# Two projections go token tile by token tile, ScalarE's rounding moves, GpSimd makes some remainders

## The chip, the core and the metric

The kernel runs on one core of a Trainium2 chip. A core has a matrix engine (TensorE, PE in the rows; its weight loads are PEld), a vector engine (VectorE, DVE), an activation engine (ScalarE, ACT), a general engine (GpSimd, POOL) and a sync engine (SyncE, SP) that issues most transfers. The metric is the device time of one execution in microseconds, the median of three runs.

## The reference, cut to what matters

A first block (mixer, memory attention, 32 experts, a final rmsnorm) is followed by a second block of two layers. All tensors are 256 tokens by 1024 features.

```python
x = first_block(...)              # ends with x + moe_ffn(h), then rmsnorm(x, norm_final)
for layer in range(2):
    shift, scale, gate = ada_modulation(c, ada_w[layer, 0], ada_b[layer, 0])
    h = x * (1.0 + scale) + shift
    if layer % 2 == 0:
        y = mixer_ab(h, ...)      # begins with h @ w_in, 1024 x 1224
    else:
        y = mixer_c(h, ...)       # begins with h @ w_in, 1024 x 3072
    x = layer_norm(DN_ALPHA * x + gate * y, ...)
    shift, scale, gate = ada_modulation(c, ada_w[layer, 1], ada_b[layer, 1])
    h = x * (1.0 + scale) + shift
    y = squared_relu_mlp(h, mlp_w1[layer], mlp_w2[layer])
    x = layer_norm(DN_ALPHA * x + gate * y, ...)
```

The change touches the two lines `h @ w_in`. In the kernel the four uses of a modulated `h` are counted 0 to 3: the first (`a` = 0, "m0", weights `ab_in`), the MLP of layer 0 (1), the third (`a` = 2, "m2", weights `c_in`) and the last MLP (3).

## The kernel before

The 256 tokens are two token tiles t of 128, the 1024 features eight chunks k of 128. A product in full precision is made of three products of rounded numbers: each operand is split into a rounded part ("hi", type fp32r) and a remainder ("lo" = value minus hi), and `three` (L1185 is its matmul line) adds hi·hi, hi·lo and lo·hi into one PSUM bank.

**Weights** stream in granules of 2 MB through a ring of slots. ScalarE makes the rounded part (`split_hi`, L535) and VectorE the remainder (`split_lo`, L545); the counts w_hi and w_lo tell TensorE what is ready. `ab_in` is three granules: chunks 0 to 2, 3 to 5, and 6 and 7. The first granule's remainder is made in three pieces of 1224 columns by VectorE (`ab_in_lo`, L2271). `c_in` is six granules of four chunks; the first projection of m2 uses granules 0 and 1.

**Activations.** When the normalized X of a token tile is there (`xhat`), `transpose_hat` (L1689) turns 8 chunks of it on TensorE; the banks 4 to 7 hold two chunks of both tiles each, so a bank is complete only with the second tile. Then `evac_hi` on ScalarE (L960) makes the modulated and rounded part XT_r, one instruction of 256 columns for a chunk, and `evac_lo` on VectorE the remainder: two instructions from bank and XT_r into sb_XN (L2461), two from sb_XN into the remainder's place (L2466), four times. A chunk's matmuls wait for both.

**Around m0.** Behind the last expert ScalarE rounds `ab_in` 0, loads the table for the square root (L915), rounds `ab_in` 1, and then squares and sums X tile by tile (L919, L922). VectorE first adds the experts' banks to X (L2262), then makes the first piece of remainder, then 1/root and the scaled X (L2277, L2278: `xhat`), and further pieces between the rest. `keep_busy(0, 2)` (L1176) are matmuls without use.

**Around m2.** `layer_norm(1, ...)` on VectorE is, for each tile and half, bank times gate (L2411), plus X (L2412: both inputs in SBUF), statistics (L2413), and then small ones that alternate with ScalarE's root (L940). The first tile is scaled by ScalarE (`ln_hat`, L947), the first half of the second by VectorE (L2422). ScalarE rounds `c_in` 1 before the layer norm's first root; VectorE makes the remainders of `c_in` 1 to 3 behind `evac_lo(2)`.

The order on every engine is that of the code; semaphores join the engines. GpSimd is idle between 276.13 us, its last instruction of the routing, and 1246.25 us.

## Time and profile before

| | us |
|---|---|
| median of three runs | 1863.99 (1863.71 to 1864.62) |
| the profiled execution | 1861.1, of which its trace spans 1859.3 |
| TensorE busy | 1760.3 (95%) |
| VectorE busy | 741.1 (40%) |
| ScalarE busy | 533.5 (29%) |
| GpSimd busy | 28.1 (2%) |
| m0: from the last expert's last ScalarE instruction to the end of the projection | 1193.75 to 1238.10 |
| m2: from the end of the MLP's matmuls to the end of the first two `c_in` granules | 1525.11 to 1555.65 |

Shares over the whole span hide the two stretches; they are read from timelines of single engines, where each row gives its start, how long the group took, and, in brackets, how long the engine had been idle and who ended that. The chain of waits says which of the engines decides the end.

### The profile page before, as it was taken

The page shows a single profiled execution, that of the slowest core. Times are in us where ns is not written, and L with a number is a line of the kernel's source. Part 1 is how long each engine was busy: PE and PEld are TensorE (multiplying, and loading weights), DVE is VectorE, ACT ScalarE, POOL GpSimd, SP SyncE. Part 2 cuts the span into 40 slices and gives each one's busy share as a digit, 9 for nine tenths or more (in the row PEclk, how much of TensorE's full clock was granted, in tenths as well). Part 3 has the DMA queues.
Part 4 walks back from the last instruction along what each step waited for, and adds up shares of the span by engine and source line. Part 5 has one row for each costly group of instructions (what it writes and reads, how often), then busy time and mean ns, then how long its engine had stood idle before and what let it go on. Part 6 is the DMA issues. An engine that isn't in the chain of part 4 may idle for free.

```text
span 1859.3 us, 24433 instructions
## 1 busy us (share of the span) xinstructions
PE 1760.3 (95%) x9970; PEld 1105.8 (59%) x9970; DVE 741.1 (40%) x1253; ACT 533.5 (29%) x693; POOL 28.1 (2%) x33
## 2 busy tenths in 40 slices
PE   6999999999999999999999999798899999989997
PEld 6787774344344343443434434375699878679986
DVE  3245352122122121221212212278865568675545
ACT  4344430110110110101111010327544452644442
POOL 0101000000000000000000000000000000000001
PEclk9999999999999999999999999998999999999999
DMA  9767799999999999999999999954345555435550
GB/s 328 286 234 273 278 374 427 428 428 428 428 429 429 429 428 429 429 429 429 429 429 428 429 429 429 413 213 179 114 178 184 200 185 191 171 114 181 180 203 23
DMA packets 96698, 587.60 MB, mean 316 GB/s; under 512 B 7118, under 2 KB 7332, under 8 KB 71044
## 3 DMA queue, kind: packets, MB, share of 16 engines
q1 hardware_dynamic: 95348, 582.12, 77.4%
q10 hardware_dynamic: 1296, 4.72, 0.8%
q8 instruction: 39, 0.64, 0.1%
q14 instruction: 15, 0.12, 0.0%
HBM read 585.77 MB, written 1.05 MB: 316 GB/s over the span
## 4 chain that ended last, share of the span: by engine, by line
PE 73%; DMA 19%; DVE 4%; ACT 3%; issue 1%; SPq 0%; ACTq 0%; DVEq 0%
PE bank L1185 35%; DMA ring<-in_w_gate_up 18%; PE bank L1468 15%; PE bank L1487 8%; PE bank L1426 4%; PE bank L1498 1%; PE bank L1274 1%; PE bank L1460 1%; ACT arena L899 1%; PE bank L1480 1%; PE bank L1259 1%; PE bank L1646 1%; PE bank L1633 0%; PE bank L1388 0%; PE bank L1828 0%
## 5 line engine op out<-in xcount | busy, mean ns | idle before, releaser
L1468 PE MATMUL bank<-ring,arena 128*64 128x512 f32 x2048 | 463.1, 598 | 27.4 <-DMA ring<-in_w_gate_up 26.9
L1468 PEld LDWEIGHTS bank<-ring,arena 128*64 128x64 f32 x2048 | 138.1, 137 | 319.8 <-issue 258.0
L1185 PE MATMUL bank<-w_hi,arena_r 128*128 128x512 f32 (+1 forms) x784 | 257.4, 390 | 4.7 <-DVE arena_r L2312 2.8
L1487 PE MATMUL bank<-ring,arena 128*64 128x512 f32 x1024 | 226.8, 595 | 3.4
L545 DVE TENSOR_TENSOR w_lo<-ring,w_hi 128x4096 fp32r<-128x4096 f32 (+2 forms) x43 | 188.1, 4375 | 53.1 <-ACT w_hi L535 50.9
L535 ACT ACTIVATE w_hi<-ring 128x4096 fp32r<-128x4096 f32 (+2 forms) x45 | 159.0, 3572 | 45.5 <-DMA ring<-in_c_w_out 25.5
L897 ACT ACTIVATE arena<-arena,sb_tab 128x512 f32<-128x512 f32 x32 | 23.1, 722 | 513.3 <-DVE arena L2167 513.3
L1185 PEld LDWEIGHTS bank<-w_hi,arena_r 128*128 128x128 f32 x784 | 147.7, 188 | 35.2 <-DVE arena_r L2312 3.3
L2167 DVE TENSOR_SCALAR arena<-bank 128x512 f32<-128x512 f32 x32 | 22.1, 692 | 366.7 <-PE bank L1468 366.7
L1487 PEld LDWEIGHTS bank<-ring,arena 128*64 128x64 f32 x1024 | 72.0, 137 | 137.6 <-issue 132.7
L1185 PE MATMUL bank<-XT_r,w_hi 128*128 128x256 f32 x512 | 146.6, 286 | 4.4 <-DVE arena_r L2466 4.4
L1185 PE MATMUL bank<-arena_r,w_hi 128*128 128x256 f32 x512 | 145.6, 284 | 0.0
L1185 PE MATMUL bank<-XT_r,w_lo 128*128 128x256 f32 x512 | 145.5, 284 | 0.0
L1426 PEld LDWEIGHTS bank<-arena,sb_XN 128*128 128x128 f32 x1056 | 123.2, 192 | 26.0 <-issue 26.0
L1426 PE MATMUL bank<-arena,sb_XN 128*128 128x64 f32 x1056 | 128.4, 275 | 0.0
L1185 PE MATMUL bank<-w_lo,arena_r 128*128 128x512 f32 x320 | 125.0, 391 | 0.0
L2188 DVE SCALAR_TENSOR_TENSOR arena_r<-bank,sb_att,arena_r 128x512 fp32r<-128x512 f32 x32 | 24.0, 751 | 217.4 <-ACT arena_r L902 217.4
L1185 PEld LDWEIGHTS bank<-XT_r,w_hi 128*128 128x128 f32 x512 | 98.9, 193 | 5.8 <-issue 5.3
L1185 PEld LDWEIGHTS bank<-arena_r,w_hi 128*128 128x128 f32 x512 | 99.0, 193 | 0.9 <-issue 0.5
L1185 PEld LDWEIGHTS bank<-XT_r,w_lo 128*128 128x128 f32 x512 | 98.9, 193 | 0.0
L902 ACT ACTIVATE arena_r<-bank,sb_att 128x512 fp32r<-128x512 f32 x32 | 22.0, 687 | 231.2 <-PE bank L1487 231.2
L522 DVE TENSOR_TENSOR half_lo<-ring,half_hi 128x2048 fp32r<-128x2048 f32 x24 | 55.0, 2291 | 82.7 <-ACT half_hi L512 82.6
(389 smaller groups left out, 2104.4 us busy)
## 6 DMA issues: line engine op xcount, KB each, us to landing
ring<-in_w_gate_up SPq DMA_DIRECT2D x128, 2048.0 KB, 32.0
ring<-in_w_down SPq DMA_DIRECT2D x64, 2048.0 KB, 35.3
ring<-in_mlp_w SPq DMA_DIRECT2D x32, 2048.0 KB, 8.3
ring<-in_ada_w SPq DMA_DIRECT2D x22, 2048.0 KB, 12.5
ring<-in_c_w_in SPq DMA_DIRECT2D x6, 2048.0 KB, 7.6
ring<-in_w_in SPq DMA_DIRECT2D x4, 2048.0 KB, 9.9
ring<-in_w_k SPq DMA_DIRECT2D x2, 2048.0 KB, 12.4
ring<-in_w_v SPq DMA_DIRECT2D x2, 2048.0 KB, 8.7
```

Of the source, the lines that this page charges most:

```text
L522: eng.tensor_tensor(lo[:], half_raw(name, h)[1], hi[:].bitcast(F32), ALU.subtract).then_inc(sem("w_lo"), 1)
L535: act.activation(pair(g)[0][:, 0:w], slot(slot_of(g), w), ACT.Copy).then_inc(sem("w_hi"), 1)
L545: eng.tensor_tensor(lo[:, 0:w], slot(slot_of(granule_no(name, i)), w), hi[:, 0:w].bitcast(F32), ALU.subtract).then_inc(sem("w_lo"), 1)
L897: act.activation(sig, gcl, ACT.Sigmoid, bias=zero, scale=1.702).then_inc(sem("e_sig"), 1)
L899: act.activation(hT, B[0][:].rearrange("p (c n) -> p c n", c=4), ACT.Copy).then_inc(sem("e_hTe"), 1)
L902: act.activation(y_hi, B[2][:], ACT.Copy, scale=slot_gate).then_inc(sem("e_y"), 1)
L1185: mm = pe.matmul(out, st[a], mv[b], start=start and a + b == 0, stop=stop and a == 1, skip_group_check=True)
L1426: mm = pe.matmul(B[3][:, k * CAP:(k + 1) * CAP], XN[:, t, k * P:(k + 1) * P], sel_tok[:, t, :], start=(t == 0), stop=(t == 1))
L1468: mm = pe.matmul(B[m][CAP * h:CAP * h + CAP, :], xe[:, 2 * j + kl, :], w[:, kl, m * D + h * HW:m * D + (h + 1) * HW], start=False, stop=(j ...
L1487: mm = pe.matmul(B[2][CAP * h:CAP * h + CAP, :], hT[:, c, CAP * j:CAP * j + CAP], w[:, c, h * HW:(h + 1) * HW], start=(j == 0 and c == 0), ...
L2167: dve.tensor_scalar(gcl, B[0][:], 7.0, None, ALU.min).then_inc(sem("e_clamp"), 1)
L2188: dve.scalar_tensor_tensor(y_lo, B[2][:], slot_gate, y_hi.bitcast(F32), ALU.mult, ALU.subtract).then_inc(sem("e_ylo"), 1)
```

## The change

For m0 and for m2's first two granules, tile 0 is transposed alone into banks 4 and 5 (`transpose_tile`), and its two kinds of evacuation are made for it alone, 128 columns each (`evac_tile`). TensorE then runs, for a granule and tile 0, all hi·hi products, all with the weights' remainder, and last those with the activations' remainder; between the second and the third comes the transposing of tile 1 into banks 6 and 7, once (`project_tiles`). In m0 tile 1's outputs take banks 4 and 5, so TensorE waits there until tile 0's remainders are all made.

ScalarE no longer rounds `ab_in` 0 inside the last expert; the expert loop runs all 32. It loads the square root's table, rounds two thirds of `ab_in` 0, does the squares, rounds the last third, evacuates tile 0, rounds `ab_in` 1, and evacuates tile 1. In m2 four of tile 0's evacuations stand before tile 1's root. The five first pieces of `ab_in`'s remainder (granule 0 and two thirds of granule 1) are GpSimd's, the sixth VectorE's behind both tiles. The remainder of `c_in` 1 is GpSimd's in one instruction of 4096 columns. `keep_busy(0, 2)` ahead of m0 is `keep_busy(0, 5)`.

```diff
+        def ab_in_lo(eng, k):
+            g = granule_no("ab_in", k // 3)
+            n, cut = split_no(g), slice(k % 3 * 1224, (k % 3 + 1) * 1224)
+            hi, lo = pair(g)
+            if k < 2:
+                eng.wait_ge(sem("ab_in_hi"), 1)
+            else:
+                eng.wait_ge(sem("w_hi"), n)
+            eng.wait_ge(sem("w_lo"), n - 1)
+            ins = eng.tensor_tensor(lo[:, cut], slot(slot_of(g))[:, cut], hi[:, cut].bitcast(F32), ALU.subtract)
+            ins.then_inc(*((sem("w_lo"), 1) if k % 3 == 2 else (sem("ab_in_part"), 1)))
...
+            for k in range(5):
+                ab_in_lo(pool, k)
             pool.wait_ge(sem("late_read"), 1)
...
+            split_lo(pool, "c_in", 1)
             pool.wait_ge(sem("late_read"), 3)
...
-            expert(NE - 1, (used, MOE_END), ("ab_in", 0))
...
             act.activation(stat[:, 59:60], eps5, ACT.Sqrt, bias=zero)
-            split_hi(act, "ab_in", 1)
...
+            ab_in_hi(0, 2)
             for t in range(TB):
                 act.wait_ge(sem("moe_x"), 2 * t + 2)
...
-            evac_hi(0)
+            ab_in_hi(2, 3)
+            evac_tile(0, 0, range(KC))
+            split_hi(act, "ab_in", 1)
+            evac_tile(0, 1, range(KC))
             split_hi(act, "ab_in", 2)
...
             ln_hat(1, 0)
+            evac_tile(2, 0, range(4))
             ln_root(1, 1)
             ln_hat(1, 1)
-
-            evac_hi(2)
+            evac_tile(2, 0, range(4, KC))
+            evac_tile(2, 1, range(KC))
...
+                for t in range(TB):
+                    for wa in range(2):
+                        for kl in range(len(ks)):
+                            term(t, 0, wa, kl)
+                    if t == 0 and second is not None:
+                        second()
+                    for kl in range(len(ks)):
+                        mm = term(t, 1, 0, kl)
+                    if t == 0 and second is not None:
+                        pe.wait_ge(*upto(f"m{a}", "xt_v", KC))
+                mm.then_inc(used, 1)
...
-            keep_busy(0, 2)
-            transpose_hat(0)
+            keep_busy(0, 5)
+            transpose_tile(0, 0)
...
+                if j:
+                    pe.wait_ge(sem("w_lo"), split_no(g))
+                if j == 1:
+                    pe.wait_ge(sem("ab_in_part"), 4)
...
-            ab_in_lo(0)
             for t in range(TB):
                 dve.wait_ge(*upto("fin", "root", t + 1))
                 link(dve.reciprocal(stat[:, 80 + t:81 + t], stat[:, 18 + t:19 + t]))
                 dve.tensor_scalar(X[:, t, :], X[:, t, :], stat[:, 80 + t:81 + t], None, ALU.mult).then_inc(
                     sem("xhat"), 1)
-            ab_in_lo(1)
...
+            def evac_tile(a, t):
+                g1, g0 = modcol(a)
+                for q in range(2):
+                    dve.wait_ge(*upto(f"m{a}", "xt_a", KC * t + 4 * q + 4))
+                    for k in range(4 * q, 4 * q + 4):
+                        if t:
+                            dve.wait_ge(*upto(f"m{a}", "xt_v", k + 1))
+                        ins = dve.scalar_tensor_tensor(XN[:, 0, k * P:(k + 1) * P], B[4 + 2 * t + q][:, k % 4 * P:k % 4 * P + P],
+                                                       g1(k), XT_r[:, k, t * P:(t + 1) * P].bitcast(F32), ALU.mult,
+                                                       ALU.subtract)
+                    link(ins)
+                    for k in range(4 * q, 4 * q + 4):
+                        dve.tensor_scalar(XTL[a][:, k, t * P:(t + 1) * P], XN[:, 0, k * P:(k + 1) * P], g0(k), None,
+                                          ALU.add).then_inc(sem("xt_v"), 1)
...
-            evac_lo(0)
-            split_lo(dve, "ab_in", 1)
+            for t in range(TB):
+                evac_tile(0, t)
+            ab_in_lo(dve, 5)
             rope_angles()
...
-            evac_lo(2)
-            for i in range(1, 4):
+            for t in range(TB):
+                evac_tile(2, t)
+            for i in range(2, 4):
                 split_lo(dve, "c_in", i)
```

ScalarE behind the experts in m0, the program before. w_hi_49, w_hi_51 and w_hi_53 are the rounded parts of `ab_in` 0, 1 and 2.

```order
L535 ACTIVATE w_hi_49<-ring 128x3672
...
L915 ACT_TABLE_LOAD
L915 ACTIVATE sb_stat<-sb_tab 128x1
L535 ACTIVATE w_hi_51<-ring 128x3672
L919 ACTIVATE sb_XN,sb_stat<-sb_X,sb_tab 128x1024
L922 ACTIVATE sb_stat<-sb_stat,sb_tab 128x1
L919 ACTIVATE sb_XN,sb_stat<-sb_X,sb_tab 128x1024
L922 ACTIVATE sb_stat<-sb_stat,sb_tab 128x1
L960 ACTIVATE XT_r<-bank,sb_mod 128x256 x8
L535 ACTIVATE w_hi_53<-ring 128x2448
```

The same place on ScalarE, the changed program (its line numbers are those of the changed kernel; L936 is `ab_in_hi`, L993 `evac_tile`).

```order
L929 ACT_TABLE_LOAD
L929 ACTIVATE sb_stat<-sb_tab 128x1
L936 ACTIVATE w_hi_49<-ring 128x2448
L942 ACTIVATE sb_XN,sb_stat<-sb_X,sb_tab 128x1024
L945 ACTIVATE sb_stat<-sb_stat,sb_tab 128x1
L942 ACTIVATE sb_XN,sb_stat<-sb_X,sb_tab 128x1024
L945 ACTIVATE sb_stat<-sb_stat,sb_tab 128x1
L936 ACTIVATE w_hi_49<-ring 128x1224
L993 ACTIVATE XT_r<-bank,sb_mod 128x128 x8
L535 ACTIVATE w_hi_51<-ring 128x3672
L993 ACTIVATE XT_r<-bank,sb_mod 128x128 x8
L535 ACTIVATE w_hi_53<-ring 128x2448
```

Of 7344 rounded columns ahead of the first square, 2448 are left there; 1224 stand behind the squares, and 3672 between the two tiles' evacuations.

VectorE in m0, the program before (L2271 are the pieces of remainder, L2278 is `xhat`).

```order
L2262 TENSOR_TENSOR sb_X<-bank,sb_X 128x512 x4
L2271 TENSOR_TENSOR w_lo_50<-ring,w_hi_49 128x1224
L2277 RECIPROCAL sb_stat<-sb_stat 128x1
L2278 TENSOR_SCALAR sb_X<-sb_X,sb_stat 128x1024
L2277 RECIPROCAL sb_stat<-sb_stat 128x1
L2278 TENSOR_SCALAR sb_X<-sb_X,sb_stat 128x1024
L2271 TENSOR_TENSOR w_lo_50<-ring,w_hi_49 128x1224
L2461 SCALAR_TENSOR_TENSOR sb_XN<-bank,sb_mod,XT_r 128x256 x2
L2466 TENSOR_SCALAR arena_r<-sb_XN,sb_mod 128x256 x2
L2271 TENSOR_TENSOR w_lo_50<-ring,w_hi_49 128x1224
```

The same place on VectorE, the changed program.

```order
L2340 TENSOR_TENSOR sb_X<-bank,sb_X 128x512 x4
L2344 RECIPROCAL sb_stat<-sb_stat 128x1
L2345 TENSOR_SCALAR sb_X<-sb_X,sb_stat 128x1024
L2344 RECIPROCAL sb_stat<-sb_stat 128x1
L2345 TENSOR_SCALAR sb_X<-sb_X,sb_stat 128x1024
L2524 SCALAR_TENSOR_TENSOR sb_XN<-bank,sb_mod,XT_r 128x128 x4
L2529 TENSOR_SCALAR arena_r<-sb_XN,sb_mod 128x128 x4
```

The pieces of remainder have left this queue; the evacuations follow `xhat` directly, four of each kind in a row.

GpSimd between the routing and the last layer norm, the difference of the two programs.

```order
+L744 TENSOR_TENSOR sb_mod<-sb_mod,sb_col 128x8
+L559 TENSOR_TENSOR w_lo_50<-ring,w_hi_49 128x1224 x3
+L559 TENSOR_TENSOR w_lo_52<-ring,w_hi_51 128x1224 x2
+L750 TENSOR_TENSOR sb_mod<-sb_mod,sb_ada_bT 128x8
+L752 TENSOR_TENSOR sb_mod<-sb_mod,sb_ada_bT 128x16
+L754 TENSOR_TENSOR sb_stat<-sb_mod,sb_col 128x8
+L756 TENSOR_TENSOR sb_mod<-sb_mod,sb_stat 128x8
+L757 TENSOR_TENSOR sb_mod<-sb_mod,sb_col 128x8
+L545 TENSOR_TENSOR w_lo_54<-ring,w_hi_53 128x4096
+L760 TENSOR_TENSOR sb_mod<-sb_mod,sb_ada_bT 128x8
```

Five subtractions of 1224 columns and one of 4096 have come in between the small ones that were there.

## Rows read from the trace of the kernel before

**Rows 1.** The page: its chain of waits by engine, whole span.

```profile
PE 73%; DMA 19%; DVE 4%; ACT 3%; issue 1%; SPq 0%; ACTq 0%; DVEq 0%
```

**Rows 2.** Chain of waits, both projections: start us, us, what ran, count.

```profile
1212.86 25.24 PE bank L1185 x135
...
1531.98 67.15 PE bank L1185 x288
```

**Rows 3.** Timeline of ScalarE, first projection: start us, us, engine, line, tiles, count.

```profile
1193.75 0.69 ACT L902 ACTIVATE arena_r<-bank,sb_att 128x512 fp32r<-128x512 f32 x1 [7.25 <-PE bank L1487]
1194.34 3.26 ACT L535 ACTIVATE w_hi<-ring 128x3672 fp32r<-128x3672 f32 x1
1197.61 1.28 ACT L915 ACT_TABLE_LOAD   x1
...
1199.11 3.25 ACT L535 ACTIVATE w_hi<-ring 128x3672 fp32r<-128x3672 f32 x1
1202.26 1.13 ACT L919 ACTIVATE sb_XN<-sb_X,sb_tab 128x1024 f32<-128x1024 f32 x1
...
1207.35 3.75 ACT L960 ACTIVATE XT_r<-bank,sb_mod 128x256 fp32r<-128x256 f32 x8 [2.08 <-PE bank L1689]
1210.95 2.28 ACT L535 ACTIVATE w_hi<-ring 128x2448 fp32r<-128x2448 f32 x1
```

**Rows 4.** Timeline of VectorE, the same stretch.

```profile
1196.83 2.48 DVE L2262 TENSOR_TENSOR sb_X<-bank,sb_X 128x512 f32<-128x512 f32 x4 [1.60 <-PE bank L1498]
1199.23 1.42 DVE L2271 TENSOR_TENSOR w_lo<-ring,w_hi 128x1224 fp32r<-128x1224 f32 x1
...
1204.05 0.75 DVE L2278 TENSOR_SCALAR sb_X<-sb_X,sb_stat 128x1024 f32<-128x1024 f32 x1
...
1208.40 0.88 DVE L2461 SCALAR_TENSOR_TENSOR sb_XN<-bank,sb_mod,XT_r 128x256 f32<-128x256 f32 x2 [0.80 <-ACT XT_r L960]
1209.32 0.62 DVE L2466 TENSOR_SCALAR arena_r<-sb_XN,sb_mod 128x256 fp32r<-128x256 f32 x2
```

**Rows 5.** Timeline of TensorE, the same stretch.

```profile
1196.66 1.98 PE L1176 MATMUL bank<-sb_tab 128*128 128x512 f32 x4
1204.86 3.50 PE L1689 MATMUL bank<-sb_tab,sb_X 128*128 128x128 f32 x16 [6.21 <-DVE sb_X L2278]
```

**Rows 6.** Windows: stretch, length, busy times of engines, granted clock (PEclk), DMA, GB/s.

```profile
1204.80:1209.80 5.00, 3.50 (x16) 3.27 (x17) 3.63 (x8) 2.89 (x9) 0.00 (x0) 0.68 0.92 340
...
1533.00:1534.00 1.00, 1.00 (x4) 0.71 (x4) 1.00 (x4) 1.00 (x2) 0.00 (x0) 0.50 0.00 0
```

**Rows 7.** GpSimd: one group of the groups by line, then its timeline.

```profile
L522 POOL TENSOR_TENSOR half_lo<-ring,half_hi 128x2048 fp32r<-128x2048 f32 x4 | 18.4, 4602 | 165.4 <-ACT half_hi L512 165.4
...
1848.93 2.36 POOL L746 TENSOR_TENSOR sb_X<-sb_X,arena 128x1024 f32<-128x1024 f32 x1 [216.35 <-ACT sb_X L947]
1851.37 2.67 POOL L748 TENSOR_TENSOR sb_X<-sb_X,arena 128x1024 f32<-128x1024 f32 x1
```

**Rows 8.** Timeline of VectorE in the last 10 us, beside GpSimd.

```profile
1849.78 0.69 DVE L2411 TENSOR_TENSOR sb_XN<-bank,sb_XN 128x512 f32<-128x512 f32 x1 [0.22 <-PE bank L1185]
1850.51 1.33 DVE L2412 SCALAR_TENSOR_TENSOR sb_X<-sb_X,sb_XN 128x512 f32<-128x512 f32 x1
...
1853.50 1.08 DVE L2428 SCALAR_TENSOR_TENSOR sb_X<-sb_X,sb_att,arena 128x512 f32<-128x512 f32 x1
```

**Rows 9.** Third projection: timelines of ScalarE, of VectorE, of TensorE.

```profile
1514.51 3.61 ACT L535 ACTIVATE w_hi<-ring 128x4096 fp32r<-128x4096 f32 x1
...
1517.97 0.69 DVE L2412 SCALAR_TENSOR_TENSOR sb_X<-sb_X,sb_XN 128x512 f32<-128x512 f32 x1
...
1520.59 0.69 DVE L2412 SCALAR_TENSOR_TENSOR sb_X<-sb_X,sb_XN 128x512 f32<-128x512 f32 x1
...
1528.39 0.54 DVE L2422 TENSOR_SCALAR sb_X<-sb_X,sb_att 128x512 f32<-128x512 f32 x1
...
1525.11 1.03 PE L1689 MATMUL bank<-sb_tab,sb_X 128*128 128x128 f32 x8
```

More of the change, by code:

```diff
@@ L892, in _, with expert @@
             ada(1)
-            def expert(i, down_done, ahead=None):
+            def expert(i, down_done):
                 act.wait_ge(sem("e_clamp"), 2 * i + 1)
@@ L1694, in transpose_hat, with transpose_tile, project_tiles, term @@
                         keep_busy(0, 3)
+            def transpose_tile(a, t):
+                st = "fin" if a == 0 else f"ln{a - 1}"
+                if a == 0:
+                    pe.wait_ge(*upto(st, "xhat", t + 1))
+                elif t == 0:
+                    pe.wait_ge(*upto(st, "xhat_a", 1))
+                else:
+                    pe.wait_ge(*upto(st, "xhat", 1))
+                for k in range(KC):
+                    if a and t == 1 and k == 4:
+                        pe.wait_ge(*upto(st, "xhat_a", 2))
+                    mm = pe.transpose(B[4 + 2 * t + k // 4][:, k % 4 * P:k % 4 * P + P], X[:, t, k * P:(k + 1) * P], ident)
+                    if k % 4 == 3:
+                        mm.then_inc(sem("T"), 1)
+            def project_tiles(a, g, w, ks, outs, width, second=None, w_ready=None):
+                def term(t, xa, wa, kl):
+                    k = ks[kl]
+                    pe.wait_ge(*upto(f"m{a}", ("xt_a", "xt_v")[xa], KC * t + k + 1))
+                    if t + xa == 0 and w_ready is not None:
+                        w_ready(wa, kl)
+                    x = (XT_r, XTL[a])[xa]
+                    for c, b in enumerate(outs[t]):
+                        mm = pe.matmul(b, x[:, k, t * P:(t + 1) * P], w[wa][:, kl, width * c:width * c + width],
+                                       start=k + xa + wa == 0, stop=xa == 1 and k == KC - 1, skip_group_check=True)
+                    return mm
+                for t in range(TB):
[9 more added lines that the diff above has]
+                mm.then_inc(used, 1)
             def x_chunk(a, k):
```

72 lines of the change are left out of this document (34 added, 38 removed).

## The prediction

> **What bounds the kernel now.** I read the chain of waits first: TensorE holds 73% of it [rows 1], and in both places that the change touches the chain lies on the projection's matmuls once they run: 135 of the 144 of m0 from 1212.86 to 1238.10, 0.187 us each, and 288 of m2 from 1531.98, 0.233 us each [rows 2]. Their number does not change, so a gain can come only from an earlier start or fewer gaps. Ahead of them the bound is a relay, read from the timelines. In m0 it runs: the last expert's end 1194.44, rounding of `ab_in` 0 for 3.26, table 1.28, rounding of `ab_in` 1 for 3.25, first square at 1202.26 [rows 3]; then root, `xhat` at 1204.05 on VectorE [rows 4], transposing at 1204.86 [rows 5], evacuation from 1207.35. In m2 it is VectorE's layer norm up to 1528.93, then transposing and evacuation until 1531.98 [rows 9, 2].
>
> **m0, ScalarE.** Without the two roundings ahead, the table load follows the last expert at about 1195.0 (0.5 us for the count that it must read, an estimate), ends 1196.3, the root's warm-up 1196.5, two thirds of `ab_in` 0 (2448 columns cost 2.28 [rows 3]) 1198.8. The first square can start then: its X half tiles are added by 1198.1 (two of the four of 2.48 us [rows 4]). So 1198.7 against 1202.26: **3.5 us earlier**. The last third of `ab_in` 0 stands behind the second root, 1201.6 to 1202.8. Evacuating costs 0.46 us per 256 columns (3.75 for 8); 128 columns lie between half and all of that; I take 0.35, so 2.9 us a tile, as the fixed part weighs more than the columns. Rounding `ab_in` 1 between the tiles costs 3.26 and ends about 1209.0.
>
> **m0, without a collision.** The relay's fixed distance from square to transposing is 2.6 us (1202.26 to 1204.86), so transposing at 1201.3. The longer `keep_busy` (10 instructions; 4 cost 1.98 [rows 5], so 4.6) ends by 1201.2 and is hidden in the wait; would X come earlier, it would cost the overlap. TensorE then works on hi·hi and hi·lo of tile 0, waits for GpSimd's third piece, and would end about 1233.0: **5.1 us gained**, if GpSimd and VectorE ran side by side.
>
> **GpSimd's price, and whom it stops.** A GpSimd subtraction of 2048 columns costs 4.60, one of 1024 costs 2.36 [rows 7]: 1224 cost 2.8, 4096 cost 9.1. VectorE pays 1.42 for 1224 [rows 4]. But the last 10 us of the trace show more. VectorE's L2412, with two SBUF inputs, takes 0.69 everywhere [rows 9], yet 1.33 at 1850.51, and ends at 1851.84: GpSimd's first operation ran until 1851.29 [rows 7, 8]. L2428 takes 1.08 and ends 1854.58, GpSimd's second having ended at 1854.04. Both end 0.55 behind GpSimd, which is their own streaming: they stood still until it was through. The second GpSimd operation is 0.31 longer than the first, since it in turn met the running L2412. L2411, from a bank and one SBUF tile, ran in the middle of it in 0.69: not stopped. So **two-input SBUF operations of VectorE and GpSimd exclude each other for a whole instruction**. L2278 and L2466 have one SBUF tile as input; no row shows them beside GpSimd. L2278 makes 1024 columns in 0.75, twice the rate per column of L2271, so it must move two columns at a time; I take it and L2466 as stopped too, and the bound on the other side is that they are not (a rival).
>
> The page "SBUF — State Buffer" of the Trainium skill, section "SBUF: two separate sides", says that the pair of ports that GpSimd and VectorE share is an exclusive lock, held for the whole instruction, and that a VectorE operation in a 2-port performance mode takes it as well. By that rule L2278 and L2466 are stopped, and the sum is the one below; without it the sum would be that of the second rival.
>
> **m0 with the collision.** GpSimd piece 1: 1198.85 to 1201.65. `xhat` 0 wants to start at 1200.45, starts streaming at 1201.65, done 1202.2; transposing at 1202.3. Piece 2: to 1205.0; `xhat` 1 waits for it, done 1205.6. Piece 3: to 1208.4. TensorE needs it for the last hi·lo products of tile 0: done 1209.0, tile 1 transposed 1210.0, the remainder products 1211.7. Tile 0's remainders on VectorE: the first four that read the bank (L2461's kind) pass freely, the four from sb_XN (L2466's kind) wait for piece 3: 1209.1. Piece 4 (its rounded input is there at 1209.05) holds 1209.1 to 1211.95, and the second four want 1210.3. After it either all four go ahead of piece 5, and are done 1212.6, or one goes and three wait until 1214.95, done 1215.4. Behind that are tile 1's evacuations (a pair of 256 columns costs 0.88 from the bank and 0.62 from sb_XN [rows 4]; at two thirds of that each for 128 columns, eight of each cost about 3.8 us) and the sixth piece, 1.42. The granule's w_lo is thus complete at 1219.2 or 1220.7, and TensorE, through with granule 0 by 1217.6 or 1220.4, needs it for the other 90 matmuls, 16.8 us: end 1236.0 or 1237.5, against 1238.10. **I take 1.0 us gained**, nearer to the second, for a waiting piece seems to find the gaps between four short operations. The low clock (0.68 in the stretch before the first matmuls [rows 6]) falls into the waits for GpSimd here.
>
> The downstream `ab_in` 2 remainder is needed 10 us after granule 1 begins and stands 6 us behind the sixth piece: hidden. SyncE's fills follow TensorE's counts and move with them.
>
> **m2 without a collision.** Tile 0 is transposed at 1525.1 as before [rows 9]; with its evacuation ready at 1526.7, 16 products (3.7 us) fill the time in which VectorE finishes tile 1 (1528.93). The 96 matmuls would take 22.4 from about 1527, plus 1.0 for the second transposing: end near 1551 against 1555.65, **4.5 gained**.
>
> **m2 with the collision.** ScalarE finishes rounding `c_in` 1 at 1518.12 [rows 9]. VectorE's L2412 of tile 0, first half, runs 1517.97 to 1518.66; GpSimd's 9.1 us operation then holds 1518.6 to 1527.7. The next L2412 wants 1520.59 [rows 9] and stands until 1527.7: it ends 1528.25 instead of 1521.28. **Every later step of the layer norm is 7.0 us later**: tile 0's X at 1531.3, tile 1's first half at 1535.9 instead of 1528.93. TensorE has nothing from 1525.3 to 1531.3 (the transposing that had run there waits). As in m0 before, where 6.2 us of idle time stood ahead of a granted clock of 0.5 until 1208.5, 3.6 us into the work, I count the first 3.6 us at the 1.2 GHz level. Transposing 1531.35 to 1533.1; 16 products until 1537.7; tile 1 transposed 1538.6; 8 products 1540.4; tile 1's 24 with VectorE's evacuations just ahead, 1545.9; the second granule 48 x 0.23: 1556.9. Against 1555.65, where a low clock of 0.5 around 1533 [rows 6] was paid as well: **1.2 us lost**, between 0.5 (clock stays high) and 3 (GpSimd gets in ahead of the first L2412, whose start is only 0.2 us before the release). The four evacuations before tile 1's root end before that root is due, so they cost nothing. The 4.4 us that VectorE is spared behind are not on the path: `c_in` 2 is needed after 1556.
>
> **Sum.** -1.0 + 1.2 = +0.2 us on the profiled span of 1859.3; the execution lies 1.8 above its span and the median 2.9 above that, both unchanged. Predicted: 1863.99 + 0.2 = **1864.2**.
>
> **Rivals.**
> *The full gain* (10%): neither collision matters, -5.1 - 4.5: 1854.4. For it speaks that GpSimd is idle there; against it the two stretched rows.
> *Only two-input operations are stopped* (12%): m0 gains most, -5.0 + 1.2: 1860.2. No row contradicts it; the double rate of L2278 does.
> *GpSimd keeps the port from piece to piece* (15%), the slow side: pieces 1 to 3 queue without a gap, 1198.85 to 1207.3, and `xhat` 0 waits for all, transposing at 1208.1; later pieces 4 and 5 do the same and piece 6 is done at 1225, so m0 ends 1241.8, +3.7, with m2 +1.2: 1868.9. It decides as soon as the second piece is let in ahead of a VectorE operation that already waits. Against it: at 1851.3 the waiting L2412 went first, though GpSimd's next had a semaphore to wait for.
> *GpSimd gets in first in m2* (8%): L2412 is stopped already at 1517.97, 1.7 us more: 1865.9.
> The forecast has 55%.
>
> **How the numbers follow.** A measurement of this kernel can tell about 0.2%, 3.7 us, from no change. The forecast's own spread is 1861 to 1867.5. The range takes in the second and third rival, 1859.5 to 1869.0, and leaves out the full gain and tails. Faster by over 0.2% (below 1860.3): the full gain, half of the second rival, the forecast's tail, 0.23. Slower (above 1867.7): the third rival and tails, 0.23. Same: 0.54.
>
> **What would show it.** In the changed trace: the square at 1198.7; `xhat` 0 stretched to about 1.7 us and `xhat` 1 to more; the four operations from sb_XN standing until a GpSimd piece ends; TensorE idle between 1206 and 1208.5; the sixth piece done near 1220; in m2 one L2412 of about 7.7 us, and TensorE idle some 6 us with a granted clock of 0.5 behind it. I am wrong if these operations keep their lengths, if GpSimd's pieces differ from 2.8 and 9.1, or if the table load does not follow the experts at once.

## The result, and the profile after

The changed kernel takes 1867.71 us (median of 17, 1865.61 to 1871.94), the kernel before 1863.57 beside it (median of 17, 1859.75 to 1872.54). The ratio is 1.0023, 95% interval 1.0014 to 1.0031: slower by 2.6 to 5.8 us. Forecast were +0.2 us and, as the likeliest case (0.54), a time within 3.7 us of the kernel before. The range of 1859.5 to 1869.0 held the time; it lies at the border of the case "slower" (above 1867.7), which had 0.23. A second series of the same pair gave 1.0022 (1.0012 to 1.0031).

The chain of waits by engine, whole span (for [rows 1]):

```profile
PE 71%; DMA 19%; DVE 4%; ACT 4%; issue 1%; SPq 0%; ACTq 0%; DVEq 0%
```

The chain in the two projections, changed kernel (start us, us, what, count; for [rows 2]; L1758 is the matmul of `project_tiles`, L1222 that of `three`):

```profile
1202.65 3.11 DVE sb_X L2345
...
1206.84 2.27 DVE arena_r L2529 x4
...
1212.31 3.21 DVE arena_r L2529 x3
1215.56 23.52 PE bank L1758 x117
...
1521.73 7.47 DVE sb_X L2478
...
1534.23 5.04 PE bank L1758 x16
...
1540.15 18.16 PE bank L1758 x80
1558.31 32.65 PE bank L1222 x144
```

New on it are exactly the VectorE operations that stood still: `xhat` of tile 1, the second step of tile 0's remainders, and one addition of the layer norm.

ScalarE in m0 (timeline; for [rows 3]; L936 rounds `ab_in` 0, L942 is the first square, L993 `evac_tile`):

```profile
1194.32 0.69 ACT L919 ACTIVATE arena_r<-bank,sb_att 128x512 fp32r<-128x512 f32 x1 [7.19 <-PE bank L1524]
1195.41 1.28 ACT L929 ACT_TABLE_LOAD   x1 [0.41 <-issue]
...
1199.05 1.13 ACT L942 ACTIVATE sb_XN<-sb_X,sb_tab 128x1024 f32<-128x1024 f32 x1
...
1203.36 2.90 ACT L993 ACTIVATE XT_r<-bank,sb_mod 128x128 fp32r<-128x128 f32 x8 [0.19 <-PE bank L1745]
```

VectorE in m0 (timeline; for [rows 4]):

```profile
1200.83 1.72 DVE L2345 TENSOR_SCALAR sb_X<-sb_X,sb_stat 128x1024 f32<-128x1024 f32 x1
...
1202.65 3.11 DVE L2345 TENSOR_SCALAR sb_X<-sb_X,sb_stat 128x1024 f32<-128x1024 f32 x1
1205.69 1.11 DVE L2524 SCALAR_TENSOR_TENSOR sb_XN<-bank,sb_mod,XT_r 128x128 f32<-128x128 f32 x4
1206.84 2.27 DVE L2529 TENSOR_SCALAR arena_r<-sb_XN,sb_mod 128x128 fp32r<-128x128 f32 x4
...
1210.17 5.34 DVE L2529 TENSOR_SCALAR arena_r<-sb_XN,sb_mod 128x128 fp32r<-128x128 f32 x4
```

GpSimd, whose five pieces ran beside it (for [rows 7]):

```profile
1199.21 9.21 POOL L559 TENSOR_TENSOR w_lo<-ring,w_hi 128x1224 fp32r<-128x1224 f32 x3 [924.47 <-ACT w_hi L936]
1209.49 5.54 POOL L559 TENSOR_TENSOR w_lo<-ring,w_hi 128x1224 fp32r<-128x1224 f32 x2 [1.06 <-ACT w_hi L535]
```

`xhat` took 0.75 before and takes 1.72 and 3.11 now. The first ends at 1202.55, 0.57 behind GpSimd's first piece (1199.21 to 1201.98). The reads from a bank (L2524) kept 1.11 for four beside the same pieces; the four of L2529, 0.87 where GpSimd is idle, took 2.27 and 5.34.

TensorE behind that (timeline; for [rows 5]):

```profile
1208.58 0.80 PE L1758 MATMUL bank<-w_lo,XT_r 128*128 128x408 f32 x3 [1.65 <-POOL w_lo L559]
...
1215.56 3.10 PE L1758 MATMUL bank<-w_hi,XT_r 128*128 128x408 f32 x9 [3.65 <-DVE arena_r L2529]
```

The window behind it (for [rows 6]; stretch, length, busy time and count of PE, PEld, DVE, ACT and POOL, granted clock, DMA share, GB/s):

```profile
1216.00:1219.00 3.00, 3.00 (x11) 2.90 (x10) 2.93 (x14) 0.24 (x1) 0.00 (x0) 0.50 0.00 0
```

Nine matmuls take 3.10 us right behind the wait and 1.83 to 1.94 elsewhere: the granted clock is 0.50, which is 1.2 GHz.

GpSimd ahead of m2 (timeline):

```profile
1519.33 9.30 POOL L545 TENSOR_TENSOR w_lo<-ring,w_hi 128x4096 fp32r<-128x4096 f32 x1 [218.45 <-ACT w_hi L535]
```

VectorE's layer norm beside it (for [rows 9]; L2478 adds X, both inputs in SBUF; L2479 makes the statistics from one):

```profile
1519.84 0.69 DVE L2479 BATCH_NORM_STATS2 sb_rt<-sb_X 128x6 f32<-128x512 f32 x1
1521.01 0.69 DVE L2477 TENSOR_TENSOR sb_XN<-bank,sb_XN 128x512 f32<-128x512 f32 x1 [0.48 <-PE bank L1222]
1521.73 7.46 DVE L2478 SCALAR_TENSOR_TENSOR sb_X<-sb_X,sb_XN 128x512 f32<-128x512 f32 x1
```

And TensorE, which waits for it through ScalarE:

```profile
1532.26 1.97 PE L1745 MATMUL bank<-sb_tab,sb_X 128*128 128x128 f32 x8 [5.85 <-ACT sb_X L970]
```

One GpSimd instruction covers three VectorE operations. Two pass in their usual 0.69; the third stands until GpSimd is through at 1528.6 and ends 0.56 behind it. TensorE waits 5.85 us, and then transposes at half speed (1.97 for eight, 1.03 elsewhere).

**Stages.** The table is worked out, from landmarks in the timelines of every traced kernel. m0 runs from the end of the last expert's last ScalarE operation (1194.44 before) to the first copies of its result (1238.12). "To LN0" goes on to the layer norm's first statistics, "MLP 0" to those ahead of m2 (1518.70). m2 runs from there to the end of the first two `c_in` granules (1555.65), "attention" from VectorE's first operation in the last attention (1606.65) to the projection behind it (1635.01). Stages that hardly differ are left out. Medians and ratios are of all executions; the stages are those of one trace each. A ratio is against the executions of the kernel before in the same series, whose median moved between 1862.6 and 1864.1, and it is not the quotient of two medians: for both_on_vector, where two of eight executions took 1853, the medians give 0.9981.

| kernel | m0 | to LN0 | MLP 0 | m2 | attention | median | ratio |
|---|---|---|---|---|---|---|---|
| before | 43.7 | 91.3 | 189.3 | 36.9 | 28.4 | 1863.6 | |
| before_again | 44.1 | 93.1 | 189.3 | 36.9 | 28.4 | | |
| before_c_gpsimd | 44.3 | 93.2 | 189.3 | 43.3 | 28.4 | 1870.1 | 1.0028 |
| changed | 44.1 | 91.4 | 189.3 | 38.5 | 29.9 | 1867.7 | 1.0023 |
| after_again | 45.6 | 91.0 | 190.6 | 38.4 | 30.0 | 1866.6 | 1.0022 |
| c_on_vector | 43.9 | 89.5 | 190.7 | 35.2 | 30.2 | 1866.4 | 1.0016 |
| ab_on_vector | 41.1 | 93.4 | 189.3 | 38.5 | 29.9 | 1864.2 | 0.9997 |
| both_on_vector | 41.2 | 92.2 | 190.7 | 35.2 | 29.9 | 1860.6 | 0.9964 |
| both_kept_busy | 41.1 | 89.5 | 189.3 | 35.1 | 28.4 | 1858.6 | 0.9971 |
| c_gpsimd_pieces | 44.9 | 90.9 | 190.6 | 32.8 | 28.4 | 1861.2 | 0.9993 |
| late_remainder_gpsimd | 45.4 | 90.9 | 190.5 | 38.4 | 30.0 | 1868.2 | 1.0020 |
| late_remainder | 37.4 | 94.7 | 190.8 | 30.8 | 29.8 | 1847.6 | 0.9906 |
| late_again | 37.4 | 89.6 | 190.6 | 30.8 | 29.9 | 1850.9 | 0.9947 |
| late_gpsimd_pieces | 37.4 | 93.1 | 190.8 | 32.8 | 28.4 | 1851.3 | 0.9936 |

The traces settle m2 to 0.1 us for one and the same work. They settle m0 as well where GpSimd makes none of its pieces (41.1 and 41.2, or 37.4), but not where it makes five: the changed kernel, after_again, c_on_vector and c_gpsimd_pieces have the same m0 and take 43.9 to 45.6. The other stages do the same work in every kernel and still vary by 1.3 to 5 us. Their length follows the clock: "to LN0" has a mean granted clock of 0.94 in late_again (89.6), 0.93 before (91.3) and 0.89 in late_remainder (94.7).

### The profile page after: what moved, and what is told of

The parts are those of the page before. It is cut to its first block, busy times and chain, and to the rows that moved or that the text cites. A ratio compares the mean times of both kernels' runs of the same rounds, so it can differ in the third digit from the quotient of the medians.

```text
span 1863.5 us, 24489 instructions
## 1 busy us (share of the span) xinstructions
PE 1763.4 (95%) x9970; PEld 1106.7 (59%) x9970; DVE 749.7 (40%) x1281; ACT 539.3 (29%) x711; POOL 52.2 (3%) x39
## 4 chain that ended last, share of the span: by engine, by line
PE 71%; DMA 19%; DVE 4%; ACT 4%; issue 1%; SPq 0%; ACTq 0%; DVEq 0%
PE bank L1222 31%; DMA ring<-in_w_gate_up 18%; PE bank L1505 15%; PE bank L1524 8%; PE bank L1463 4%; PE bank L1758 3%; PE bank L1535 1%; PE bank L1311 1%; PE bank L1497 1%; ACT arena L916 1%; PE bank L1517 1%; PE bank L1296 1%; PE bank L1683 1%; DVE sb_X L2478 1%; PE bank L1670 1%
## 5 line engine op out<-in xcount | busy, mean ns | idle before, releaser
L1222 PE MATMUL bank<-w_hi,arena_r 128*128 128x512 f32 x704 | 227.3, 392 | 4.7 <-DVE arena_r L2378 2.8
L545 DVE TENSOR_TENSOR w_lo<-ring,w_hi 128x4096 fp32r<-128x4096 f32 (+1 forms) x41 | 179.7, 4383 | 54.2 <-ACT w_hi L535 51.6
L535 ACT ACTIVATE w_hi<-ring 128x4096 fp32r<-128x4096 f32 (+2 forms) x44 | 155.8, 3581 | 38.5 <-DMA ring<-in_c_w_out 25.4
L1222 PEld LDWEIGHTS bank<-w_hi,arena_r 128*128 128x128 f32 x704 | 132.2, 188 | 33.8 <-DVE arena_r L2378 3.3
L1222 PE MATMUL bank<-XT_r,w_hi 128*128 128x256 f32 x512 | 146.5, 286 | 4.4 <-DVE arena_r L2546 4.4
L1222 PE MATMUL bank<-arena_r,w_hi 128*128 128x256 f32 x512 | 145.5, 284 | 0.0
L1222 PE MATMUL bank<-XT_r,w_lo 128*128 128x256 f32 x512 | 145.5, 284 | 0.0
L1222 PE MATMUL bank<-w_lo,arena_r 128*128 128x512 f32 x320 | 124.9, 390 | 0.0
L1222 PEld LDWEIGHTS bank<-XT_r,w_hi 128*128 128x128 f32 x512 | 99.0, 193 | 5.8 <-issue 5.3
L1222 PEld LDWEIGHTS bank<-arena_r,w_hi 128*128 128x128 f32 x512 | 99.0, 193 | 0.9 <-issue 0.5
L1222 PEld LDWEIGHTS bank<-XT_r,w_lo 128*128 128x128 f32 x512 | 98.9, 193 | 0.0
## 6 DMA issues: line engine op xcount, KB each, us to landing
ring<-in_ada_w SPq DMA_DIRECT2D x22, 2048.0 KB, 12.8
```

What stands on the lines that cost most here:

```text
L535: act.activation(pair(g)[0][:, 0:w], slot(slot_of(g), w), ACT.Copy).then_inc(sem("w_hi"), 1)
L545: eng.tensor_tensor(lo[:, 0:w], slot(slot_of(granule_no(name, i)), w), hi[:, 0:w].bitcast(F32), ALU.subtract).then_inc(sem("w_lo"), 1)
L1222: mm = pe.matmul(out, st[a], mv[b], start=start and a + b == 0, stop=stop and a == 1, skip_group_check=True)
```

## The experiments

### Who makes the remainders

The first three undo GpSimd's share of the changed kernel, one stage at a time and then both.

```diff
-            split_lo(pool, "c_in", 1)
...
-            for i in range(2, 4):
+            for i in range(1, 4):
                 split_lo(dve, "c_in", i)
```

> The changed kernel with the remainder of c_in 1 back on VectorE, behind both tiles' evacuations; everything else as changed. Theory of the port (GpSimd's subtraction stops VectorE's operations that have only SBUF inputs, for its whole length): the stretched addition of the layer norm (7.46 us) is back at 0.69, TensorE's gap of 5.8 us between the two tiles' work shrinks to under 1.5, the first two granules end 5 to 7 us earlier than in the changed kernel, and the time is about 1861.5 (1860 to 1863.5), 4 to 7 below the changed kernel. Rival of the order (the tile-by-tile order and the low clock behind a gap cost what was lost, whoever makes the remainder): within 1.5 us of the changed kernel, 1866 to 1868, and the end of the stage where it was or later, since VectorE has 4.4 us more to do ahead of granule 1.

Measured: ratio 1.0016 (1.0004 to 1.0028). m2 is 3.3 us shorter, less than the 5 to 7 that I expected, and the median only 1.3 below the changed kernel's. By its time the run lies in the range of the rival (1866 to 1868); only the stage speaks against that rival. The stop is gone, but a wait has taken its place (timeline of TensorE; VectorE's L545 is now `c_in` 1):

```profile
1540.77 2.73 PE L1757 MATMUL bank<-w_hi,XT_r 128*128 128x512 f32 x8 [2.49 <-DVE w_lo L545]
```

```diff
-            for k in range(5):
-                ab_in_lo(pool, k)
...
+            ab_in_lo(dve, 0)
             for t in range(TB):
                 dve.wait_ge(*upto("fin", "root", t + 1))
...
-            for t in range(TB):
-                evac_tile(0, t)
-            ab_in_lo(dve, 5)
+            ab_in_lo(dve, 1)
+            ab_in_lo(dve, 2)
+            evac_tile(0, 0)
+            ab_in_lo(dve, 3)
+            ab_in_lo(dve, 4)
+            evac_tile(0, 1)
+            ab_in_lo(dve, 5)
```

> The changed kernel with all six pieces of ab_in's remainder on VectorE: one ahead of the normalized X, two behind it, two between the tiles' evacuations, one behind. GpSimd keeps c_in 1. Theory of the port: the two normalized tiles take 0.75 us each (1.72 and 3.11 in the changed kernel), the first is done about 1 us earlier, the second 3 us earlier, TensorE's waits of 1.5 and 3.9 us shrink, the stage m0 ends 4 to 6 us earlier, near 1234, and the time is about 1863 (1861.5 to 1865). Rival of VectorE's load (six pieces of 1.42 us in its queue cost as much as the stops did): within 1.5 us of the changed kernel, and the sixth piece done at 1220 or later. Rival of the order: the same.

Measured: ratio 0.9997 (0.9985 to 1.0009), m0 3.0 us shorter than in the changed kernel, less than the 4 to 6 that I expected, and 2.6 to 3.2 shorter than in the three traces with the m0 of before. The first `xhat`, beside no GpSimd piece, is back at its length (timeline of VectorE):

```profile
1200.96 0.75 DVE L2344 TENSOR_SCALAR sb_X<-sb_X,sb_stat 128x1024 f32<-128x1024 f32 x1
```

> The tile-by-tile order alone: GpSimd makes no remainder at all (both edits of the two kernels before together). Theory of the port: the two savings add, since the stages are 280 us apart: about 1857.5 (1855 to 1860), 6 below the kernel before. The predicted 5.1 and 4.5 without a collision would give 1854. Rival of the order: 1865 to 1868, slower than before, and the reordering itself is what cost the time. If m0 and m2 together give under 3 us against the kernel before, the relay from the experts to the projection was sized wrongly in the prediction, not only the collision.

Measured: 1860.58, ratio 0.9964 (0.9948 to 0.9980), just above the 1855 to 1860 that I expected. The rival of the order falls: token tile by token tile alone is faster than before, and GpSimd's help turned it into a loss. But the two stages together give 4.6 us (44.0, the mean of the three traces with the order of before, to 41.2, and 36.9 to 35.2), not the 9.6 of the prediction's sums without a collision. TensorE in m0, timeline:

```profile
1215.64 1.94 PE L1755 MATMUL bank<-w_hi,arena_r 128*128 128x408 f32 x9 [0.45 <-DVE arena_r L2527]
1219.52 2.67 PE L1755 MATMUL bank<-w_hi,XT_r 128*128 128x408 f32 x9 [1.94 <-DVE w_lo L559]
1221.98 2.72 PE L1755 MATMUL bank<-w_lo,XT_r 128*128 128x408 f32 x9
1224.54 1.82 PE L1755 MATMUL bank<-w_hi,arena_r 128*128 128x408 f32 x9
```

Ahead of the second granule TensorE waits 1.94 us for its remainder, and then pays 0.85 and 0.90 more for 18 matmuls at the low clock. That is 3.7 us, and 4.3 in m2 (2.49 and some 1.8).

The opposite edit, alone on the kernel before:

```diff
+            split_lo(pool, "c_in", 1)
             pool.wait_ge(sem("late_read"), 3)
...
-            for i in range(1, 4):
+            for i in range(2, 4):
                 split_lo(dve, "c_in", i)
```

> The kernel before with one edit: GpSimd makes the remainder of c_in 1, at the point of its queue where the changed kernel has it. Theory of the port: the order of before depends on the layer norm's second tile for every matmul, so the whole stop of some 7 us is paid: the addition behind the first is 7 to 8 us long, the matmuls of m2 start 7 us later with a low clock in the first of them, and the time is 1870.5 (1869 to 1873). Without that theory (GpSimd runs beside VectorE freely): the same time as before or up to 1 us less, as the remainder isn't on the path: 1862.5 to 1864.

Measured: 1870.14, ratio 1.0028 (1.0018 to 1.0037). m2 is 6.4 longer. VectorE, timeline:

```profile
1524.03 0.69 DVE L2412 TENSOR_TENSOR sb_XN<-bank,sb_XN 128x512 f32<-128x512 f32 x1 [0.48 <-PE bank L1186]
1524.76 7.46 DVE L2413 SCALAR_TENSOR_TENSOR sb_X<-sb_X,sb_XN 128x512 f32<-128x512 f32 x1
```

With nothing else changed, the same operation stands for the same time: the collision is its own cause. It costs 6.4 us in the order that needs both tiles, and 3.3 net in the new one (38.5 against 35.2).

### The low clock behind a wait

```diff
                 g = at[0]
+                if j:
+                    keep_busy(4, 5)
                 project_tiles(2, g, chunks(split_granule(), 4), range(4 * j, 4 * j + 4),
```

> The tile-by-tile order without GpSimd, and five matmuls without use that fill TensorE's wait of 2.5 us for the remainder of c_in 1 in m2. Theory of the clock (the idle time brings the low clock): the wait stays, the eight products behind it take 1.98 us and not 2.73 and 3.04, m2 is 33.4 in place of 35.2 from the first statistics to the end of the two granules, and the time is 1.8 under the same kernel without the five, near 1858.5. Rival (the clock falls whatever TensorE does there): m2 stays 35.2.

Measured: ratio 0.9971 (0.9959 to 0.9982), m2 35.1 for an expected 33.4: no gain. That the median, 1858.61, met the expected 1858.5 is luck. The trace shows that I had made the filling too long, while the clock did what the theory says (timeline of TensorE; L1210 is `keep_busy`):

```profile
1534.42 4.46 PE L1210 MATMUL bank<-sb_tab 128*128 128x512 f32 x10
1538.32 2.40 PE L1755 MATMUL bank<-w_hi,XT_r 128*128 128x512 f32 x8
1540.55 1.98 PE L1755 MATMUL bank<-w_lo,XT_r 128*128 128x512 f32 x8
```

Each of the five lies in the trace as two, 4.46 us in all, where the wait was 2.49. Of the matmuls behind it the first eight take 2.40, still beside the last of the filling, and the next eight 1.98 where they took 3.07: the clock has stayed high, and the two effects cancel. For the clock the experiment speaks, for the time it was badly sized.

### GpSimd's one instruction in eight

```diff
-            split_lo(pool, "c_in", 1)
+            g = granule_no("c_in", 1)
+            n, (hi, lo) = split_no(g), pair(g)
+            pool.wait_ge(sem("w_hi"), n)
+            pool.wait_ge(sem("w_lo"), n - 1)
+            for k in range(8):
+                cut = slice(k * 512, (k + 1) * 512)
+                ins = pool.tensor_tensor(lo[:, cut], slot(slot_of(g))[:, cut], hi[:, cut].bitcast(F32), ALU.subtract)
+            ins.then_inc(sem("w_lo"), 1)
```

> The changed kernel with GpSimd's remainder of c_in 1 in eight instructions of 512 columns in place of one of 4096. Theory of the port (held for one instruction, and given to the other side between two): no VectorE operation is stopped for more than 1.3 us; three to five are stopped, the second tile's statistics end some 3 us later than without GpSimd and not 6.4; GpSimd ends about 1532; m2 from the first statistics to the end of the two granules is near 35.5 (38.5 in the changed kernel), the time about 1864.5. Rival (GpSimd keeps the port from piece to piece): one stop of about 7.5 us as before, m2 38.5, the time 1867.7.

Measured: ratio 0.9993 (0.9982 to 1.0004), m2 32.8, 5.6 shorter than with one instruction. VectorE, timeline:

```profile
1523.77 1.02 DVE L2485 SCALAR_TENSOR_TENSOR sb_X<-sb_X,sb_XN 128x512 f32<-128x512 f32 x1
...
1527.16 1.83 DVE L2485 SCALAR_TENSOR_TENSOR sb_X<-sb_X,sb_XN 128x512 f32<-128x512 f32 x1
...
1530.34 1.58 DVE L2485 SCALAR_TENSOR_TENSOR sb_X<-sb_X,sb_XN 128x512 f32<-128x512 f32 x1
```

GpSimd, timeline:

```profile
1521.37 11.71 POOL L764 TENSOR_TENSOR w_lo<-ring,w_hi 128x512 fp32r<-128x512 f32 x8 [219.73 <-ACT w_hi L535]
```

No operation stands for more than 1.14 us (1.83 less its own 0.69), less than one piece (11.71 for eight). So the stop lasts for one instruction and no longer, and the rival that GpSimd keeps the port from piece to piece falls. It is faster than the 35.5 that I expected: in this trace TensorE's longest wait in m2 is 0.70 us, none of its waits is for `c_in` 1, and every eight products take 1.98 to 2.11.

### The weights' remainder last

The wait that stayed in both_on_vector is not on data that TensorE needs first. In the second granule of each stage the products with the weights' remainder go behind those with the activations' remainder, and only then is that remainder waited for. All remainders are VectorE's again; the edit of m2's wait, left out here, is of the same kind:

```diff
+                if late:
+                    for t in range(TB):
+                        for xa, wa in ((0, 0), (1, 0), (0, 1)):
+                            if wa and t == 0:
+                                if a == 0:
+                                    pe.wait_ge(sem("ab_in_part"), 4)
+                                pe.wait_ge(sem("w_lo"), split_no(g))
+                            for kl in range(len(ks)):
+                                mm = term(t, xa, wa, kl)
+                    mm.then_inc(used, 1)
+                    return
...
-                    pe.wait_ge(sem("w_lo"), split_no(g))
-                if j == 1:
-                    pe.wait_ge(sem("ab_in_part"), 4)
+                    pe.wait_ge(sem("w_hi" if j == 1 else "w_lo"), split_no(g))
...
```

> All remainders on VectorE, and in both stages the second granule's products go in another order: for each token tile first rounded by rounded, then the activations' remainder, and last the weights' remainder, whose wait now stands 18 (m0) or 16 (m2) matmuls later. Theory (what is left of the loss without GpSimd is TensorE's wait for the weights' remainder, 1.94 us in m0 and 2.49 in m2, and the low clock behind each, some 1.7 us): both waits go, m0 from 43.7 us (before) to 37.6 from the last expert to the end of the projection, m2 from 37.0 to 31.5 from the layer norm's first statistics to the end of the two granules; the time is about 1853.5 (1851 to 1857), 7 under the same kernel without this edit. Rival (VectorE's queue is the bound, so the wait only comes later in the granule): 2 us or less under it, with idle time in front of the products of the weights' remainder.

Measured: 1847.61 (four times only), ratio 0.9906 (0.9887 to 0.9925); m0 37.4 and m2 30.8, 0.2 and 0.7 better than the theory said, and a time below its range (1851 to 1857). Once more, for a firmer time:

> Once more the fastest kernel so far (all remainders on VectorE, the products of the weights' remainder last in the second granules), which had only four times. From its first trace m0 and m2 are 12.6 us shorter together than before, its median was 16 lower. If the two stages are all of it: about 1851.5, ratio 0.9932. If something else gains too: 1847 to 1849, ratio 0.991 to 0.992, and then some stage that no edit touches is shorter than in both traces of before.

Measured: 1850.93 (six times), ratio 0.9947 (0.9927 to 0.9968). The two intervals do not touch. The edits don't explain it, since both traces have the same m0 and m2; what differs is "to LN0" (94.7 and 89.6). Why the two series differ is open. What the two stages give by the traces, 12.8 us (44.0 to 37.4 and 36.9 to 30.8), is a ratio of 0.9931, between the two that were measured. Both series are faster than both kernels. TensorE in m2, timeline of late_again:

```profile
1518.09 2.09 PE L1755 MATMUL bank<-w_hi,XT_r 128*128 128x512 f32 x8 [0.26 <-ACT XT_r L990]
...
1528.33 1.98 PE L1755 MATMUL bank<-w_hi,arena_r 128*128 128x512 f32 x8
1530.14 1.98 PE L1755 MATMUL bank<-w_hi,XT_r 128*128 128x512 f32 x8
1531.95 1.98 PE L1755 MATMUL bank<-w_hi,arena_r 128*128 128x512 f32 x8
1533.77 1.98 PE L1755 MATMUL bank<-w_lo,XT_r 128*128 128x512 f32 x8
```

Behind the 0.26 in the first line TensorE waits no more in m2, and every eight take 1.98 to 2.10 us.

The same order with GpSimd's remainders as in the changed kernel:

> The same new order of the second granules, but GpSimd makes the remainders as in the changed kernel. Theory of the port: m2 does not gain, since TensorE's gap there is the layer norm's second half tile and stands ahead of granule 1 (38.5 us again); m0 gains 1 to 2.5 from the sixth piece that comes late. The time is about 1866 (1864 to 1868). Rival (the remainders' lateness was the whole loss, the stops cost nothing): as fast as with VectorE, about 1855.

Measured: 1868.24, ratio 1.0020 (1.0007 to 1.0033), m2 38.4 and m0 45.4. The rival, some 1855, falls: late remainders alone were not the loss. The 1 to 2.5 us that I expected of m0 did not show, but one trace can't settle that: beside after_again, whose clock behind the wait was as low (0.63, here 0.65, over 7 us), m0 is 0.2 shorter.

> The fastest kernel so far with the remainder of c_in 1 in eight pieces of 512 columns on GpSimd. VectorE is spared 4.4 us behind both tiles' evacuations, and has its layer norm stopped in short pieces. Theory of the port: with the late order nothing waits for VectorE's 4.4 us, so only the stops are left, and m2 is 32.7 in place of 30.6 from the layer norm's first statistics to the end of the two granules; 2 us slower than that kernel. Rival (the spared VectorE time still counts, as its evacuations of tile 1 or the later remainders come earlier): 30.6 or less, same or faster.

Measured: ratio 0.9936 (0.9920 to 0.9951). The times (median 1851.25) can't tell it from late_again, the trace can: m2 is 32.8 against 30.8, the 2 us of the stops. The VectorE time that it spares is worth nothing there.

### Second traces of the two kernels

> The kernel before as it is, for a second trace of it. Theory (the stages that the change does not touch vary by single stretches of low clock, about 1.4 us each, whatever the kernel): m0 43.7 to 44.3 and m2 36.9 to 37.1 again, while the stages from m0's end to the first layer norm, over the first MLP, and over the last attention may differ from the first trace by 1.4 us each. Rival (the last attention takes 28.4 us with the order of before and 29.9 with the new one): 28.4 here.

> The changed kernel as it is, for a second trace and more times. Theory: m0 43.8 to 44.9, m2 38.2 to 38.5, the last attention 28.4 or 29.9, ratio to the kernel before 1.0015 to 1.003. Rival (the new order brings the low clock into the last attention): 29.9 there again.

m2 repeats to 0.1 us in both. m0 does not quite: 43.7 and 44.1 before (44.3 in before_c_gpsimd, the same there), 44.1 and 45.6 in the changed one, where this time four of L2529 took 6.03 us and TensorE waited 4.36. Behind that wait the clock was low for longer; the 7 us from its end, first trace and second (windows, columns as above):

```profile
1215.56:1222.56 7.00, 7.00 (x29) 6.89 (x30) 6.69 (x25) 0.68 (x1) 0.00 (x0) 0.76 0.01 2
```

```profile
1220.71:1227.71 7.00, 7.00 (x25) 6.91 (x26) 6.69 (x25) 0.08 (x1) 0.00 (x0) 0.63 0.01 2
```

In c_on_vector this clock was 0.80 and m0 43.9, in c_gpsimd_pieces 0.63 and 44.9. The second trace is of the slowest of its twelve executions (1872.44, median 1866.58), so it is not the typical one.

The first MLP of the changed kernel took 189.3 and 190.6. The same stretch, 12 us behind the layer norm's first statistics, in the first trace and in the second (windows, columns as above):

```profile
1342.50:1346.50 4.00, 2.66 (x22) 2.69 (x23) 3.89 (x13) 2.36 (x6) 0.00 (x0) 1.00 0.39 157
```

```profile
1348.00:1352.00 4.00, 2.63 (x12) 2.66 (x13) 3.89 (x12) 2.40 (x6) 0.00 (x0) 0.60 0.38 158
```

Nearly equal busy times, but 22 matmuls at a granted clock of 1.00 and 12 at 0.60. It is the same program, and in the 2 us ahead TensorE was busy for 1.09 us in both. Inside the stretch lies a wait of TensorE of 2.17 us, which every one of the fourteen traces has: in the eight with 190.5 us or more for MLP 0 the matmuls behind it ran at the low clock first (0.64 over 4 us in after_again), in the six with 189.3 they did not (1.00 in the changed kernel's first trace). The last attention shows it again, changed kernel and both_kept_busy some 7 us ahead of its end:

```profile
1632.00:1636.00 4.00, 4.00 (x23) 2.86 (x22) 1.70 (x4) 1.89 (x4) 0.00 (x0) 0.57 0.00 0
```

```profile
1624.00:1628.00 4.00, 4.00 (x36) 3.41 (x36) 1.83 (x5) 3.05 (x12) 0.00 (x0) 1.00 0.00 0
```

So a stretch of low clock, 1.3 to 1.9 us dear, comes or doesn't come in stages that no edit touches. both_kept_busy, short in both stages, has its own just ahead of that attention: from m2's end to its start it takes 53.0 us, both_on_vector 51.0, and the other twelve 50.8 to 51.2 (windows, both_kept_busy, then both_on_vector):

```profile
1549.78:1602.78 53.00, 49.84 (x237) 41.79 (x238) 34.43 (x38) 18.19 (x16) 0.00 (x0) 0.97 0.65 238
```

```profile
1556.19:1607.22 51.03, 48.38 (x238) 40.21 (x238) 34.38 (x37) 17.87 (x16) 0.00 (x0) 1.00 0.69 247
```

For the attention the number of the rival came both times: 28.4 in the order of before, and 30.0 for 29.9 in the changed kernel.

## Why the prediction was right or wrong, point by point

**ScalarE's relay: right.** The first square came at 1199.05 for 1198.7, the table load 0.41 us behind the last expert for an assumed 0.5, an evacuation of 128 columns cost 0.36 for 0.35. Counted from the last expert's end the square is 3.8 us earlier.

**The collision: right, and shown.** `xhat` 0 was 1.72 long (1.7), L2478 7.46 (7.7), GpSimd's 4096 columns 9.30 (9.1), TensorE's gap in m2 5.85 (6.0). That L2278 and L2466, with one SBUF tile as input, are stopped too was taken without a row; L2345 and L2529 now show it. The reason that was given, "twice the rate per column of L2271", was read too high: 1024 columns in 0.75 against 1224 in 1.42 is 1.6 times. By the rule of the Trainium skill ("SBUF — State Buffer", "SBUF: two separate sides") a VectorE operation in a 2-port mode takes the shared ports for the whole instruction, and the traces agree, with 3.11 us for one of 0.75. No trace shows the mode itself. By the rival "only two-input operations are stopped" m0 would have been faster than before; that rival falls. So does "GpSimd keeps the port": `xhat` 0 went ahead of the second piece. GpSimd's first three pieces cost 3.07 on average, not 2.8: the first, which waited for nobody, 2.78, the other two 3.26 and 3.25.

**m0: wrong by 1.4 to 1.9.** Predicted -1.0, measured +0.4 in the first pair of traces, +0.9 over the two of the changed kernel and the three with m0 as before, and +0.6 with c_on_vector and c_gpsimd_pieces, whose m0 is the changed one too. The step that failed is "the low clock falls into the waits for GpSimd here". TensorE waited 3.65 us until 1215.56, for tile 0's last remainders, and the clock was at 1.2 GHz until about 1219.4: 1.2 us on the first nine matmuls, about 1.7 in all. These remainders were no later than I had them: in the later of my two cases they ended at 1215.4, and in the trace at 1215.5, with the last expert's end 0.6 later than before. What I left out was the price behind the wait. The clock was charged in m2 and forgotten in m0. That the wait brings the low clock was tested only in m2 (both_kept_busy); in m0 it is read from the traces.

**m2: right.** +1.2 forecast, 38.4 and 38.5 against 36.9 measured: +1.5. The length of the low clock was taken from m0 before, where it was read as lasting until 1208.5; the windows there have 0.50 up to 1208.0 and 0.96 in the half us behind. This is worth 0.2 us of the sum.

**m0 and m2 without a collision: right as a potential, wrong as a number.** -5.1 and -4.5 were claimed, -2.9 and -1.7 came in both_on_vector. I did not ask who would make the remainders if GpSimd did not stop anyone: on VectorE they come late, and TensorE waits at the second granule and pays the clock. With these waits taken away (late_remainder) the stages give -6.6 and -6.1, more than claimed.

**The sum: 4.3 measured by the ratio (4.1 between the medians), 0.2 predicted.** That the range held the time is partly luck: its upper end, 1869.0, was set by the rival "GpSimd keeps the port", which the traces refute, and the forecast's own spread ended at 1867.5. m0 and m2 make +0.9 and +1.5, 2.4. The rest lies in stages with the same work: in the two traces of the changed kernel MLP 0 has 189.3 and 190.6 (189.3 in all three with the order of before), the attention 29.9 and 30.0 (28.4 in all three). These add 0.6 and 1.6, and with them the sum is 4.6. The term that the prediction put at nothing, besides the clock in m0, is then the granted clock in relays that the change does not touch. That sum fits, but is no proof: the last expert's end (1192.8 to 1199.8 over all traces) and the stage to LN0 (89.5 to 94.7) vary by more, in both directions and in kernels of every kind.

**What stays open.** Of eleven traces with the new order, eight have the longer MLP 0 and eight the longer attention; of three with the old order, none. both_kept_busy has neither, but a stretch of low clock just ahead of the attention instead. So each of the eleven has at least one such stretch from MLP 0 to the attention outside m2, and none of the three has one. It points at the new order, but three traces are few, and no experiment here changes the clock in one of these stages alone. Nothing here says what decides where the stretch comes.
